# Tile order and lane placement in the recurrent tails of a hybrid decoder layer (HGRN2 and gated DeltaNet)

## The chip, the cores and the metric

The kernel runs on one core of one Trainium2 chip. Its time is the device time of one execution in microseconds; a lower time is better. Before the change three runs gave 1239.63, 1239.65 and 1236.88 us, median 1239.63. The engines are TensorE (PE), VectorE (DVE), ScalarE (ACT), GpSimd (POOL) and SyncE (SP), which issues most of the DMAs.

## The reference

One decoder layer is computed for a prompt of 512 tokens and for 8 sampled sequences of 4 tokens (32 sample tokens), with shared weights. The mixer projects the input once and splits it among four groups of heads of width 256: block-sparse attention, Mamba-2, HGRN2 and gated DeltaNet. Their outputs are concatenated, go through one output projection, then follow cross-attention over 256 memory tokens and a SwiGLU block. The two recurrences that the change touches are:

```python
# HGRN2 (gla_chunked), one chunk
bcum = jnp.cumsum(gc, axis=1)
o = (jnp.einsum('blsh,bshv->blhv', att, vc)
     + jnp.einsum('blhk,bhkv->blhv', qc * jnp.exp(bcum), S))
S = (jnp.exp(b_last[:, 0])[..., None] * S
     + jnp.einsum('bshk,bshv->bhkv', kc * jnp.exp(b_last - bcum), vc))
# gated DeltaNet (gated_delta_chunked), one chunk; t_mat is a triangular inverse
v_new = u - jnp.einsum('bhlk,bhkv->bhlv', w, S)
o = (jnp.einsum('bhls,bhsv->blhv', qk, v_new)
     + jnp.einsum('blhk,bhkv->blhv', qc * jnp.exp(gam)[..., None], S))
S = jnp.exp(gam_h[:, :, -1])[..., None, None] * S + jnp.einsum('blhk,bhlv->bhkv', k_dec, v_new)
```

The prompt starts from a zero state; each sampled sequence starts from its own state, which is updated and returned.

## The kernel before

All 544 tokens lie side by side in the free dimension, features in the partitions. TILES cuts them into four prompt tiles of 128 tokens (0 to 3) and the sample tile of 32 tokens (4). The program of each engine is written out by hand in stages: inputs, win, ssm, gdn, wout, cross, wxo, wdn. There is no scheduler: every engine runs its instructions in the order of the code, and semaphores carry the waits between engines. Inside a stage several generators run as lanes, and a string of letters says whose step comes next on PE, DVE and ACT alike.

The ssm stage has the lanes m (Mamba-2, then HGRN2), p (the sampled attention with its pages), u (norms of the DeltaNet's q and k) and n (the Mamba norm). LANES orders them. The third step of n on DVE (ssm_norm_vector, L2165) scales Mamba's output, two instructions of 128x544; its other steps on DVE are empty. A step of p on DVE ends the softmax of the sampled attention: a reduce, a reciprocal and two scalings (L1726 to L1730), for whose result PE waits. HGRN2 computes its attention matrix by levels (j = 0 to 7): DVE scales q and k, PE multiplies, DVE places the result (place, L2348). Then comes HGRN's tail: h_kd, the decayed k, and v are turned by PE (turn, L2467) into banks 0 and 1, ACT copies them (kept), PE multiplies k and v into a state contribution (added) and the outputs (output), DVE updates the state (state, L2548). The tail takes the tiles in the order 0, 1, 4, 2, 3. The banks 0 and 1 also hold level products, hence the waits on h_lv_out.

The gdn stage begins with gdn_tensor (L2800): for each tile, products of k with k and q; DVE masks them with decays (L2706 to L2726). Between two tiles hgrn_norm_tensor (L2265) sums the squares of HGRN's outputs per head, eight PE records (an fp32 product leaves two records in the trace); it needs ACT's two squares of those outputs. Then the triangular inverses are built, a dense exchange between PE, DVE and ACT. Last comes the DeltaNet tail (gdn_tail_tensor, L2877, gdn_tail_vector, L2965), lane t, interleaved with lane k, the projection of the memory tokens to K and V: 16 GEMM steps of 24 products each, then 4 steps in which K is turned (four transposes and one ACT copy each). GDN_LANES is "tk" three times, "tkk" seven times, then "tkkk". A tile takes two t steps on PE: in the first the state is applied to the keys (tail_w) and the next tile is turned, in the second come v_new, DVE's copy of it, and then state contribution and outputs. For the sample tile the state is one per sequence: 32 products of 4 columns for tail_w, 32 more for the outputs; DVE expands v_new to one block per sequence (4 instructions of 32x512, tail_vm), and PE multiplies it in four products of 512 columns into banks 4 and 7.

G_TURNS orders the tiles 0, 4, 1, 2, 3. The four sample products of 512 columns stand behind an extra yield, so two GEMM steps run ahead of them:

```python
if x == 2:
    turn(x + 1)
yield
if sample:
    pe.wait_ge(S("tail_vm"), 3)
```

After the stage all engines meet: the wout stage is entered when PE, DVE and ACT have ended gdn.

Of the kernel before, what the change touches and what calls it, by code (L numbers as in the profile page):

```python
# [19 lines left out]
ALU = mybir.AluOpType  # L20
# [47 lines left out]
def build(nc, a, o):  # L68
# [12 lines left out]
    with ctx:  # L81
# [2252 lines left out]
        def hgrn_vector(v):  # L2334
# [112 lines left out]
        H_PLACED = sum(len(H_JOBS[j]) for j in (*range(H_PACKED), 7))  # L2447
# [18 lines left out]
        def hgrn_tail_tensor(pe):  # L2466
            def turn(i):  # L2467
                t0, w, _ = TILES[i]
                x = H_AT[i]
                if x >= 2:  # L2470
                    pe.wait_ge(S("tail_tok_out"), x - 1)
                else:
                    pe.wait_ge(S("h_lv_out"), H_PLACED - len(H_JOBS[7]) + x + 1)
# [15 lines left out]
            def output(i):  # L2489
# [4 lines left out]
                if i == 0:  # L2494
                    pe.wait_ge(S("h_lv_out"), H_PLACED)
# [49 lines left out]
        def hgrn_vector_tail(v):  # L2545
            yield
# [253 lines left out]
        def gdn_tensor(pe):  # L2800
            pe.wait_ge(S("tail_tok_out"), NT)
            pe.wait_ge(S("states_made"), 2)
            for i, (t0, w, _) in enumerate(TILES):
# [12 lines left out]
                if i == 2:  # L2816
                    hgrn_norm_tensor(pe)
# [57 lines left out]
        G_TURNS = (0, 4, 1, 2, 3)  # L2875

        def gdn_tail_tensor(pe):  # L2877
            def turn(x):

                t0, w, _ = TILES[G_TURNS[x]]  # L2880
                sl = slice(t0, t0 + w)
                b_ = bank((0, 7)[x % 2])
                if x == 3:
                    pe.wait_ge(S("states_made"), 3)
# [10 lines left out]
            for x, i in enumerate(G_TURNS):  # L2895
                t0, w, _ = TILES[i]
# [3 lines left out]
                if i and not sample:  # L2900
                    pe.wait_ge(S("tail_state"), 5 + i)
# [18 lines left out]
                if x != 2 and x + 1 < NT:  # L2920
                    turn(x + 1)
                yield
                pe.wait_ge(S("tail_tok_out"), 5 + x + 1)
# [8 lines left out]
                pe.wait_ge(S("tail_vn_out"), x + 1)  # L2932
                if not sample:
                    if i == 1:
                        pe.wait_ge(S("states_made"), 3)
# [17 lines left out]
                if x == 2:  # L2953
                    turn(x + 1)
                yield
                if sample:
# [4 lines left out]
                    last.then_inc(S("tail_st"), 1)  # L2961

        t_rt = sm(2, NS)

        def gdn_tail_vector(v):  # L2965
            yield
            for x, i in enumerate(G_TURNS):
                t0, w, _ = TILES[i]
                sl = slice(t0, t0 + w)
                sample = w == NS  # L2970
                tokens = bank((0, 7)[x % 2])
                v.wait_ge(S("tail_tok"), 5 + x + 1)
                V.tensor_copy(t_tok[0:w, 0:256], tokens[0:w, 0:256])
                if sample:
                    v.wait_ge(S("tail_w"), 1)
# [3 lines left out]
                elif i:  # L2979
                    link(V.tensor_copy(t_tok[0:w, 256:512], tokens[0:w, 256:512]))  # L2980
                    v.wait_ge(S("tail_w"), i + 1)
# [7 lines left out]
                v.wait_ge(S("tail_vn"), x + 1)  # L2989
# [625 lines left out]
```

## Time and profile before

| What | Value |
|---|---|
| time, median of 3 runs | 1239.63 us |
| time of the profiled execution | 1239.63 us |
| its span | 1238.0 us, 24845 instructions |
| DVE busy | 598.7 us (48%) |
| ACT busy | 448.9 us (36%) |
| POOL busy | 441.0 us (36%) |
| chain that ended last, by engine | PE 74%, DVE 12%, issue 4%, ACT 4% |
| HBM read, written | 131.64 MB, 10.20 MB |
| HGRN tail | about 412 to 428 us |
| start of the DeltaNet stage, up to the first inverse product | 428 to 438.6 us |
| DeltaNet tail with the memory K/V product | 481.6 to 566.4 us |

The profile is one execution recorded by the hardware profiler. Its span is the time between its first and last recorded instruction, and lies 1.6 us under the time of the same execution. Times of rows are microseconds from the span's start. PEld is TensorE's weight load, which overlaps its products. PEclk is the clock that was granted to TensorE as a share of full speed: 1.00 is 2.4 GHz, 0.50 is 1.2 GHz. A line number such as L706 can be that of a helper: L264 is every product, L267 every transpose, L706 every tensor_tensor of DVE.

### The profile page before, as it was taken

To read this page: it belongs to the slowest core of one execution; us is meant where nothing else is said; L and a number is where in the kernel's file an instruction comes from. 1 tells how busy PE (TensorE), PEld (TensorE's weight loads), DVE (VectorE), ACT (ScalarE), POOL (GpSimd) and SP (SyncE) were. 2 spreads that over 40 slices of the span, in tenths; PEclk is the share of its full clock that TensorE was granted. 3 is DMA by queue.
4 is the path that set the end of the run, shared out by engine and by line. 5 is a ranking of instruction groups with operands and counts; after the bars stand their busy time and mean duration, and the time that the engine had idled before them with its cause. 6 is when DMAs were issued, how large, how long until landed. Compare 5 with 4: busy or idle time off the path is not lost.

```text
span 1238.0 us, 24845 instructions
## 1 busy us (share of the span) xinstructions
PE 1166.6 (94%) x10272; PEld 1014.0 (82%) x10272; DVE 598.7 (48%) x1068; ACT 448.9 (36%) x802; POOL 441.0 (36%) x370
## 2 busy tenths in 40 slices
PE   7999999988988988998989899999999999999998
PEld 6999997855655688887989656988999999977775
DVE  5699735236478886413291463184433334321003
ACT  6323234245544444233552342454222223221212
POOL 8433533053417121452603200614434444433331
PEclk9999999989979998898998899999999999999999
DMA  6332523066659422336414753312222232232221
GB/s 161 91 86 69 175 74 121 2 202 183 192 156 329 134 80 81 104 107 211 120 35 141 235 174 115 104 51 86 86 86 87 85 100 82 75 103 71 83 85 72
DMA packets 176581, 143.45 MB, mean 116 GB/s; under 512 B 15955, under 2 KB 162820, under 8 KB 176214
## 3 DMA queue, kind: packets, MB, share of 16 engines
q1 hardware_dynamic: 166838, 120.44, 32.5%
q0 software_dynamic: 7200, 20.23, 5.4%
q8 instruction: 81, 1.33, 0.5%
q10 hardware_dynamic: 2432, 1.21, 0.3%
q14 instruction: 30, 0.25, 0.1%
HBM read 131.64 MB, written 10.20 MB: 115 GB/s over the span
## 4 chain that ended last, share of the span: by engine, by line
PE 74%; DVE 12%; issue 4%; ACT 4%; POOL 2%; DMA 1%; SPq 1%; POOLq 0%; DVEq 0%; ACTq 0%
PE PS L264 67%; PE PS L267 7%; DVE SC L706 2%; DVE PROJ L1939 2%; POOL W_LO L248 2%; DVE XN L936 1%; DVE XT L706 1%; DVE PROJ L2358 1%; SPq L536 1%; DVE XN L706 1%; DVE XN_parts L926 1%; ACT PROJ L1342 1%; DVE PROJ L706 1%; ACT W_HI L239 0%; DVE PROJ L1940 0%
## 5 line engine op out<-in xcount | busy, mean ns | idle before, releaser
L248 POOL TENSOR_TENSOR W_LO<-W,W_HI 128x1024 fp32r<-128x1024 f32 x128 | 313.8, 2456 | 635.1 <-ACT W_HI L239 634.9
L264 PE MATMUL PS<-XN_parts,W_HI 128*128 128x272 f32 x1184 | 340.6, 288 | 0.0
L264 PE MATMUL PS<-OM_parts,W_HI 128*128 128x272 f32 x960 | 277.3, 289 | 0.0
L264 PEld LDWEIGHTS PS<-XN_parts,W_HI 128*128 128x128 f32 x1184 | 223.2, 188 | 0.0
L239 ACT ACTIVATE W_HI<-W 128x1024 fp32r<-128x1024 f32 x128 | 134.2, 1054 | 209.5 <-PE PS L264 209.5
L264 PE MATMUL PS<-OM_parts,W_LO 128*128 128x272 f32 x704 | 203.9, 290 | 0.0
L264 PE MATMUL PS<-SC_parts,W_HI 128*128 128x272 f32 x608 | 179.9, 296 | 3.9 <-POOL W_LO L248 3.2
L264 PEld LDWEIGHTS PS<-OM_parts,W_HI 128*128 128x128 f32 x960 | 181.8, 189 | 0.1
L264 PE MATMUL PS<-SC_parts,W_LO 128*128 128x272 f32 x608 | 176.8, 291 | 0.0
L264 PEld LDWEIGHTS PS<-OM_parts,W_LO 128*128 128x128 f32 x704 | 132.3, 188 | 0.0
L264 PEld LDWEIGHTS PS<-SC_parts,W_HI 128*128 128x128 f32 x608 | 115.6, 190 | 8.3 <-issue 6.1
L264 PEld LDWEIGHTS PS<-SC_parts,W_LO 128*128 128x128 f32 x608 | 115.4, 190 | 0.0
L264 PE MATMUL PS<-W_HI,PROJ_parts 128*128 128x512 f32 (+1 forms) x320 | 110.6, 374 | 0.0
L264 PE MATMUL PS<-W_HI,SC_parts 128*128 128x256 f32 (+1 forms) x288 | 87.3, 337 | 0.0
L264 PEld LDWEIGHTS PS<-W_HI,PROJ_parts 128*128 128x128 f32 x320 | 60.9, 190 | 13.3 <-issue 2.8
L706 DVE TENSOR_TENSOR SC<-SC 128x272 f32<-128x272 f32 (+6 forms) x68 | 37.2, 550 | 50.3 <-ACT SC L866 41.1
L264 PE MATMUL PS<-OM_parts,PROJ_parts 128*128 128x272 f32 x256 | 54.7, 303 | 5.9 <-DVE XN_parts L926 3.7
L264 PEld LDWEIGHTS PS<-W_HI,SC_parts 128*128 128x128 f32 x288 | 53.1, 197 | 8.4 <-issue 4.1
L264 PE MATMUL PS<-W_LO,SC_parts 128*128 128x512 f32 (+1 forms) x160 | 58.4, 365 | 0.0
L706 DVE TENSOR_TENSOR SC<-PS,RSQ 128x544 f32<-128x544 f32 x22 | 15.9, 724 | 87.1 <-PE PS L264 85.2
L3410 ACT ACTIVATE SC<-SC 128x544 f32<-128x544 f32 x22 | 14.5, 658 | 114.9 <-DVE SC L706 114.9
L1342 ACT ACTIVATE PROJ<-PS 128x512 f32<-128x512 f32 x68 | 40.1, 598 | 40.3 <-PE PS L267 40.3
(405 smaller groups left out, 2073.7 us busy)
## 6 DMA issues: line engine op xcount, KB each, us to landing
W<-in_w_gu SPq DMA_DIRECT2D x44, 512.0 KB, 3.9
W<-in_w_in SPq DMA_DIRECT2D x30, 512.0 KB, 3.8
W<-in_w_down SPq DMA_DIRECT2D x22, 512.0 KB, 3.7
W<-in_w_xkv SPq DMA_DIRECT2D x16, 512.0 KB, 3.7
W_scratch<-in_cache_moba_v SPq DMA_DIRECT2D x36, 128.0 KB, 4.8
W_scratch<-in_cache_moba_v POOLq DMA_DIRECT2D x36, 128.0 KB, 4.9
XT<-in_cache_moba_k SPq DMA_DIRECT2D x32, 128.0 KB, 2.8
XT<-in_cache_moba_k POOLq DMA_DIRECT2D x32, 128.0 KB, 2.4
```

Of the source, the lines that this page charges most:

```text
L239: nc.scalar.activation(hi_lo(n)[0], raw_chunk(n), ACT.Copy)\
L248: nc.gpsimd.tensor_tensor(hi_lo(n)[1], raw_chunk(n), hi_lo(n)[0].bitcast(F32), ALU.subtract).then_inc(S("weights_split"), 1)
L264: return nc.tensor.matmul(out, lhsT, rhs, start=start, stop=stop, skip_group_check=True)
L267: return nc.tensor.transpose(out, in_, ident[0:k, 0:k])
L536: sp.dma_start(dst, src).then_inc(S(name), 16)
L706: return V.tensor_tensor(out, x, y, op)
L926: V.scalar_tensor_tensor(lo(k)[:, TOKENS[run][j]], XT[:, k, TOKENS[run][j]], par(GAINS[run][1] + k), hi(k)[:, TOKENS[run][j]].bitcast(F32) ...
L936: last = V.scalar_tensor_tensor(xn[:, k, c_], xn[:, k, c_], par(GAINS[run][0] + k), rsq[:, c_], ALU.mult, ALU.mult)
L1342: return A.activation(o_, i_, ACT.Copy)
L1939: V.scalar_tensor_tensor(dst[:, d:SEQ], src[:, 0:SEQ - d], wt[3 - d], dst[:, d:SEQ], ALU.mult, ALU.add)
L2358: V.copy_predicated(h_store(i, w), level.bitcast(I32), src).then_inc(S("h_lv_out"), 1)
L3410: A.activation(f_g[:, t % 2, :], f_g[:, t % 2, :], ACT.Silu).then_inc(S("ff_silu"), 1)
```

## The change

The change makes four edits; the number and the shapes of all products and vector instructions stay the same.

1. In HGRN's level loop the multiply h_kd = hk * h_d moves from ahead of the placement of level 7 to behind it and behind the two subtractions on the table lev. PE's waits on h_lv_out in the tail go, as tail_prep now comes after all placements.
2. In LANES the third step of the Mamba norm moves two main steps forward, directly ahead of the step that ends the softmax of the sampled attention.
3. hgrn_norm_tensor stands behind tile 0 of gdn_tensor and no longer behind tile 2.
4. The DeltaNet tail takes the tiles in the order 0, 1, 2, 3, 4. The sample tile's state products stand directly behind its outputs, without a yield ahead of them, and DVE's scaling of the sample states stands behind the wait for those products. The waits on states_made in PE's program go.

The core of the diff:

```diff
@@ hgrn_vector
-                if j == 7:
-                    v.wait_ge(S("tail_ebd"), 1)
-                    tt(h_kd, hk, h_d, ALU.mult).then_inc(S("tail_prep"), 1)
@@ hgrn_tail_tensor, turn and output
-                else:
-                    pe.wait_ge(S("h_lv_out"), H_PLACED - len(H_JOBS[7]) + x + 1)
-                if i == 0:
-                    pe.wait_ge(S("h_lv_out"), H_PLACED)
@@ hgrn_vector_tail
+            v.wait_ge(S("tail_ebd"), 1)
+            tt(h_kd, hk, h_d, ALU.mult).then_inc(S("tail_prep"), 1)
             yield
@@ gdn_tensor
-                if i == 2:
+                if i == 0:
                     hgrn_norm_tensor(pe)
@@ gdn_tail_tensor
-        G_TURNS = (0, 4, 1, 2, 3)
-                if x == 3:
-                    pe.wait_ge(S("states_made"), 3)
-            for x, i in enumerate(G_TURNS):
+            for i, (t0, w, _) in enumerate(TILES):
-                if x != 2 and x + 1 < NT:
-                    turn(x + 1)
+                if i + 1 < NT:
+                    turn(i + 1)
-                    if i == 1:
-                        pe.wait_ge(S("states_made"), 3)
-                if x == 2:
-                    turn(x + 1)
-                yield
                 if sample:
                     pe.wait_ge(S("tail_vm"), 3)
...
                     last.then_inc(S("tail_st"), 1)
+                yield
@@ gdn_tail_vector
-                yield
+                else:
+                    yield
...
+                v.wait_ge(S("tail_st"), 5 + i + 1)
                 if sample:
                     link(tt(t_s0.rearrange("p b c d -> p (b c) d"), t_s0.rearrange("p b c d -> p (b c) d"),
                             bc(t_lasts.rearrange("p b (c o) -> p (b c) o", o=1), (P, 2 * NB, DH)), ALU.mult))
-                v.wait_ge(S("tail_st"), 5 + x + 1)
-                if sample:
@@ LANES
-                         + ["u"] + ["ppppu"] * 4 + ["ppppuun"] * 2 + ["pppp", "p", "p", "np", "", "", ""])
+                         + ["u"] + ["ppppu"] * 4 + ["ppppuun"] * 2 + ["pppp", "np", "p", "p", "", "", ""])
```

On DVE, at the end of HGRN's levels: the first row with L706 and SC<-W is the making of h_kd, L2358 the placement of level 7, L2171 the Mamba norm, L1726 to L1730 the end of the sampled attention's softmax.

```order
-L706 TENSOR_TENSOR SC<-W 128x1088 [waits tail_ebd]
 L2358 COPY_PREDICATED PROJ<-CN,PS 128x512 [waits h_lv_out,h_lv_mm] x4
 L706 TENSOR_TENSOR CN<-CN 128x128 [waits h_lv_out]
 L706 TENSOR_TENSOR CN<-CN 128x128
-L1726 TENSOR_REDUCE SC<-SC 128x1 [waits satt_exp]
+L706 TENSOR_TENSOR SC<-W 128x1088 [waits tail_ebd]
+L2171 SCALAR_TENSOR_TENSOR OM<-OM,SM,RSQ 128x544 [waits tail_root]
+L2171 SCALAR_TENSOR_TENSOR OM<-OM,SM,RSQ 128x544
+L1726 TENSOR_REDUCE SC<-SC 128x1 [waits satt_exp,vector_chain]
 L1727 RECIPROCAL SC<-SC 128x1 [waits vector_chain]
 L1729 TENSOR_SCALAR W<-PS,SC 128x256 [waits ms_values_used,vector_chain]
 L1730 TENSOR_SCALAR W<-PS,SC 128x256 [waits vector_chain]
```

Three large instructions now stand between the placement and the softmax's reduce, where none stood; the two of L2171 stood further behind.

On PE, at the start of the gdn stage: 128x128 rows with XN,PROJ are the products of a tile, RSQ,CN and SC,CN with 128x272 the sums for HGRN's norm.

```order
 L264 MATMUL PS<-XN,PROJ 128x128 x3
 L264 MATMUL PS<-PROJ 128x128 x4
+L264 MATMUL PS<-RSQ,CN 128x272 [waits tail_sq]
+L264 MATMUL PS<-RSQ,CN 128x272
+L264 MATMUL PS<-SC,CN 128x272 x2
 L264 MATMUL PS<-XN,PROJ 128x128 [waits tail_state]
 L264 MATMUL PS<-XN,PROJ 128x128 x3
```

The sums, with their wait for ACT's squares (tail_sq), now stand ahead of the products of tile 1.

On PE, the sample tile of the DeltaNet tail before: 32x64 is v_new, 64x32 and 64x4 are the outputs, and what follows is the GEMM of the memory projection.

```order
L264 MATMUL PS<-XN,PROJ 32x64 [waits tail_tok_out]
L264 MATMUL PS<-XN,PROJ 32x64 x3
L264 MATMUL PS<-XT,XN 64x32 [waits tail_vn_out]
L264 MATMUL PS<-XT,XN 64x32 x3
L264 MATMUL PS<-SC,XN 64x4 x32
L264 MATMUL PS<-W_HI,PROJ_parts 128x256 [waits weights_split]
L264 MATMUL PS<-W_LO,PROJ_parts 128x256
```

And now, at the end of the stage, where 64x512 are the products for the sample states and the rows of L267 the turns of the memory keys:

```order
L267 MATMUL PS<-CN,PROJ 128x128 [waits kvm_out]
L267 MATMUL PS<-CN,PROJ 128x128 x3
L264 MATMUL PS<-XN,PROJ 32x64 [waits tail_tok_out]
L264 MATMUL PS<-XN,PROJ 32x64 x3
L264 MATMUL PS<-XT,XN 64x32 [waits tail_vn_out]
L264 MATMUL PS<-XT,XN 64x32 x3
L264 MATMUL PS<-SC,XN 64x4 x32
L264 MATMUL PS<-SC,XN 64x512 [waits tail_vm]
L264 MATMUL PS<-SC,XN 64x512 x3
L267 MATMUL PS<-CN,PROJ 128x128 [waits kvm_out]
L267 MATMUL PS<-CN,PROJ 128x128 x3
```

The sample tile moved from between GEMM steps to between the turns, and its 64x512 products, which wait for DVE (tail_vm), follow its outputs directly.

## Rows read from the trace of the kernel before

**Rows 1.** The page, part 1: busy time and share of each engine.
```profile
PE 1166.6 (94%) x10272; PEld 1014.0 (82%) x10272; DVE 598.7 (48%) x1068; ACT 448.9 (36%) x802; POOL 441.0 (36%) x370
```

**Rows 2.** Chain that ended last, HGRN tail: start us, us, engine, tile, line.
```profile
413.09 2.57 DVE PROJ L2358 x4
...
417.24 0.49 DVE W L1730
...
417.78 0.92 PE PS L264 x24
...
423.36 3.29 PE PS L264 x32
```

**Rows 3.** Timeline, HGRN tail: start us, us, engine, line, operation, out<-in, count.
```profile
411.89 1.28 DVE L706 TENSOR_TENSOR SC<-W 128x1088 f32<-128x1088 f32 x1
...
414.23 0.44 PE L267 MATMUL PS<-CN,SC 128*128 128x128 f32 x2
...
419.66 1.48 DVE L2171 SCALAR_TENSOR_TENSOR OM<-OM,SM,RSQ 128x544 f32<-128x544 f32 x2
```

**Rows 4.** Chain that ended last, start of the DeltaNet stage.
```profile
431.53 4.29 PE PS L264 x40
...
438.59 4.63 PE PS L264 x88
```

**Rows 5.** Timeline, start of the DeltaNet stage.
```profile
429.33 0.64 ACT L2772 ACTIVATE SC<-OM 128x544 f32<-128x544 f32 x1
...
432.62 1.18 PE L264 MATMUL PS<-RSQ,CN 128*128 128x272 f32 x4
...
433.65 1.08 PE L264 MATMUL PS<-SC,CN 128*128 128x272 f32 x4
...
435.94 1.18 DVE L706 TENSOR_TENSOR PROJ<-SC,PS 64x256 f32<-64x256 f32 x3 [0.54 <-PE PS L264]
```

**Rows 6.** Windows: stretch, its us, busy us per engine, PEclk, DMA share, GB/s.
```profile
414.75:418.20 3.45, 2.42 (x40) 1.74 (x40) 3.04 (x10) 1.94 (x4) 0.00 (x0) 1.00 0.38 105
...
438.60:442.00 3.40, 3.40 (x64) 3.40 (x64) 2.99 (x10) 3.30 (x6) 0.00 (x0) 0.51 0.57 181
476.20:479.60 3.40, 2.18 (x32) 1.90 (x32) 2.32 (x5) 3.12 (x7) 0.00 (x0) 1.00 0.02 5
479.60:486.45 6.85, 6.00 (x31) 5.84 (x32) 3.44 (x9) 3.47 (x9) 0.00 (x0) 0.50 0.59 150
...
506.90:510.30 3.40, 2.90 (x67) 2.56 (x65) 2.05 (x3) 1.06 (x1) 3.21 (x2) 1.00 0.12 22
510.30:517.20 6.90, 6.90 (x54) 6.88 (x51) 4.36 (x5) 0.64 (x2) 1.25 (x1) 0.51 0.44 144
...
568.10:575.20 7.10, 6.41 (x26) 5.52 (x26) 5.88 (x9) 3.16 (x6) 0.00 (x0) 0.52 1.02 330
```

**Rows 7.** Chain that ended last, DeltaNet tail.
```profile
508.68 21.76 PE PS L264 x200
...
533.01 6.34 PE PS L264 x56
...
539.93 7.81 PE PS L264 x64
```

**Rows 8.** Timeline: products, VectorE and ScalarE work of the two tails.
```profile
424.69 1.93 PE L264 MATMUL PS<-PROJ,SC 32*64 32x512 f32 x8
...
498.68 2.03 PE L264 MATMUL PS<-SC,XN 64*64 64x4 f32 x64
...
508.66 4.63 DVE L706 TENSOR_TENSOR SC<-XN,CN 32x512 f32<-32x512 f32 x4
...
513.47 1.22 DVE L706 TENSOR_TENSOR XN<-XN,SM 128x1024 f32<-128x1024 f32 x1
...
521.96 1.28 DVE L706 TENSOR_TENSOR XN<-XN,PS 128x512 f32<-128x512 f32 x2 [7.27 <-PE PS L264]
...
565.79 0.60 ACT L3119 ACTIVATE PROJ<-PS 128x512 f32<-128x512 f32 x1 [0.26 <-PE PS L267]
```

More of the change, by code:

```diff
@@ L2446, in build @@
         H_TURNS = (0, 1, 4, 2, 3)
-        H_PLACED = sum(len(H_JOBS[j]) for j in (*range(H_PACKED), 7))
         H_AT = {i: x for x, i in enumerate(H_TURNS)}
@@ L2873, in gdn_tensor, with turn @@
             mem_turn_tensor(pe)
-        G_TURNS = (0, 4, 1, 2, 3)
         def gdn_tail_tensor(pe):
-            def turn(x):
-                t0, w, _ = TILES[G_TURNS[x]]
+            def turn(i):
+                t0, w, _ = TILES[i]
                 sl = slice(t0, t0 + w)
-                b_ = bank((0, 7)[x % 2])
-                if x == 3:
-                    pe.wait_ge(S("states_made"), 3)
+                b_ = bank((0, 7)[i % 2])
                 for k in range(2):
@@ L2899, in gdn_tail_tensor @@
                 state = t_st[i % 2]
-                if i and not sample:
+                if i:
                     pe.wait_ge(S("tail_state"), 5 + i)
@@ L2919, in gdn_tail_tensor @@
                     last.then_inc(S("tail_w"), 1)
-                if x != 2 and x + 1 < NT:
-                    turn(x + 1)
+                if i + 1 < NT:
+                    turn(i + 1)
                 yield
-                pe.wait_ge(S("tail_tok_out"), 5 + x + 1)
+                pe.wait_ge(S("tail_tok_out"), 5 + i + 1)
                 for h in range(H):
@@ L2931, in gdn_tail_tensor @@
                 last.then_inc(S("tail_vn"), 1)
-                pe.wait_ge(S("tail_vn_out"), x + 1)
+                pe.wait_ge(S("tail_vn_out"), i + 1)
                 if not sample:
-                    if i == 1:
-                        pe.wait_ge(S("states_made"), 3)
                     for h in range(H):
@@ L2966, in gdn_tail_vector @@
             yield
-            for x, i in enumerate(G_TURNS):
-                t0, w, _ = TILES[i]
+            for i, (t0, w, _) in enumerate(TILES):
                 sl = slice(t0, t0 + w)
                 sample = w == NS
-                tokens = bank((0, 7)[x % 2])
-                v.wait_ge(S("tail_tok"), 5 + x + 1)
+                tokens = bank((0, 7)[i % 2])
+                v.wait_ge(S("tail_tok"), 5 + i + 1)
                 V.tensor_copy(t_tok[0:w, 0:256], tokens[0:w, 0:256])
                 if sample:
-                    v.wait_ge(S("tail_w"), 1)
+                    v.wait_ge(S("tail_w"), i)
                     tt(t_rt, gv[:, :, sl], bank(1)[:, 0:2 * w].rearrange("p (c l) -> p c l", l=w), ALU.subtract).then_inc(S("tail_rt"), 1)
@@ L2980, in gdn_tail_vector @@
                     link(V.tensor_copy(t_tok[0:w, 256:512], tokens[0:w, 256:512]))
-                    v.wait_ge(S("tail_w"), i + 1)
+                    v.wait_ge(S("tail_w"), i)
                     for e in range(2):
@@ L2988, in gdn_tail_vector @@
                 yield
-                v.wait_ge(S("tail_vn"), x + 1)
+                v.wait_ge(S("tail_vn"), i + 1)
                 V.tensor_copy(t_vn[0:w, :], bank(2)[0:w, 0:256]).then_inc(S("tail_vn_out"), 1)
                 if sample:
-                    v.wait_ge(S("tail_vn_out"), x + 1)
+                    v.wait_ge(S("tail_vn_out"), i + 1)
                     vm4 = t_vm[0:w, :].rearrange("p (h b d) -> p h b d", b=NB, d=DH)
@@ L3013, in gdn_tail_vector @@
                     last.then_inc(S("states_made"), 1)
+                    v.drain().then_inc(S("tail_state"), 1)
                 else:
@@ L3024, in gdn_tail_vector @@
                     outputs()
+                if sample:
+                    yield
         MEM_BANKS = (3, 6, 1, 5)
```

3 lines of the change are left out of this document (1 added, 2 removed).

## The prediction

> **What bounds the kernel now.** I read the busy shares first: TensorE (PE) is busy 94% of the span [rows 1], so time is saved or lost only where PE waits, or where its clock falls. The chain that ended last, read next, gives 74% to PE and 12% to VectorE (DVE), so a DVE step counts where the chain runs over it. The change touches three stretches, and I read each there: the HGRN tail (about 412 to 428 us), the start of the DeltaNet stage (428 to 439 us) and the DeltaNet tail, which runs interleaved with the memory K/V product (494 to 566 us).
>
> In the first, the chain goes over DVE's level-7 placing (L2358), the two scalings of the sampled attention's probabilities (the second is L1730), and from 417.78 on over PE almost without a break to the last HGRN state [rows 2]. In the second, PE carries the chain from 431.53 for 4.29 us, and DVE's masking of tile 3 starts at 435.94 only when PE's products of that tile are there [rows 4, 5]. In the third, the chain is PE except for short DVE copies [rows 7]: the GEMM steps cover everything else. Last I read the granted clock: PE mostly has 1.00 (2.4 GHz), but there are stretches at 0.50 to 0.52 (1.2 GHz), each behind a stretch in which PE was partly idle or ran very small products [rows 6]. One of them, 6.90 us at 0.51 from 510.3 on, follows the sample tile of the DeltaNet tail and lies on dense GEMM.
>
> **The change part by part.** The sum is made against the profiled execution, 1239.63 us (span 1238.0), which equals the median of the runs shown.
>
> *HGRN tail.* The multiply that makes h_kd (1.28 us) goes from ahead of the four placements (2.57 us) and the two lev subtractions to behind them. For whatever comes after all of these on DVE that is a swap and costs nothing. PE's turns, which stood at 414.23 [rows 3], need h_kd and now start near 411.9 + 2.6 + 0.5 + 1.3 = 416.4. They would run 1.1 us, their copies another 0.6 us, and PE would be through the first products and the third turn at about 419. The other edit, in the lane table, puts the two Mamba norm scalings (1.48 us together, at 419.66) ahead of the reduce that leads to L1730. Before, they ran while PE was busy with products; now L1730 ends 1.5 to 1.7 us later, at about 419.4 instead of 417.73. PE has the products of those probabilities in its queue there, with added(1), turn(2), turn(3), output(1), output(4), output(2) and the sample states behind them: the chain from 417.78 on is PE's own [rows 2], so nothing behind takes the delay up. DVE has 1.48 us less to do later, but is waiting for PE there. Term: +1.6. Bounds: +0.9, if PE uses its short idle moments between 414.2 and 417.8 (it was busy 2.42 us of 3.45 [rows 6]); +1.8 at the other end.
>
> The delayed turns open a gap: PE has nothing from about 414.3 to 416.4. Between 414.75 and 418.20 its busy time falls from 2.42 us to about 1.5 us. A comparable stretch with 2.18 of 3.40 us was followed by 6.85 us at half clock [rows 6]. If the clock falls here too, the following 3.4 to 6.9 us of small products run slower. Bounds 0 and +3.4 (what the fall at 510.3 cost, worked out below); as the present stretch with 2.42 us was not punished and this one would be thinner, I take a half chance of a short fall: +0.7.
>
> *Head norm sums at tile 0 instead of tile 2.* PE's eight records of sums against blk64 run from 432.62 to 434.7 [rows 5], 2.0 us. They need ACT's second square, which ends at 429.97 [rows 5]. Placed behind tile 0, PE reaches them at 428.9, waits 1.1 us for ACT and works 2.0 us, to 432.0; tile 1's products then end at 433.1 instead of 430.4. DVE finished tile 0 at 431.5, so it now idles 1.6 us ahead of tile 1; before, it idled 0.5 us ahead of tile 3 [rows 5], which goes. Net +1.1, and 0.1 for the last links: term +1.2. Behind the waiting PE instruction stand the products of tiles 1 to 4 and the whole triangular inversion, on which DVE and ACT wait in turn, so nothing takes it up before the chain's next PE piece at 438.59 [rows 4]. Bounds +0.5 (ACT's squares earlier relative to PE) and +1.6 (the gap before tile 3 stays).
>
> *DeltaNet tail, the sample tile last.* Instructions are the same; what lies beside them differs.
>
> (a) The stretch from 508.68 holds 200 PE records in 21.76 us [rows 7]. Its parts at full clock, from rows: 72 small records at the rate of 64 in 2.03 us [rows 8] = 2.3; two GEMM steps with a first product (56 records) 6.34; two steps with the v_new products (64 records) 7.81 [rows 7]; four state products of 512 columns (8 records) 1.93 [rows 8]. Sum 18.4, so the low clock cost 3.4 us. In the new order prompt tiles stand there, as they do from 530 on, where the chain shows no such slowing. Term: -3.4. Bounds -3.4 and 0.
>
> (b) The sample tile's expansion of v_new takes DVE 4.63 us [rows 8]. Before, two GEMM steps stood in PE's queue ahead of the state products that wait for it. Now they stand directly behind the 36 output products (2.3 + 0.1 us), with no step between: PE waits 4.63 + 0.05 - 2.4, term +2.2. Behind that wait stand three of the four turns of the memory keys. Bounds +2.0 and +2.8 (DVE's copy and semaphore added).
>
> (c) The small products and the wait now make some 5.9 us of thin work (v_new 0.65, copy 0.5, outputs 2.4, wait 2.3) close to the end of the stage. The same small products with GEMM around them were enough for the fall at 510.3 (PE busy 2.90 of 3.40 us ahead of it [rows 6]). So I expect the clock to fall by the time the 512-column products run, 1.93 us at full clock and twice that at half; the turns add a little. Bounds 0 and +2.4; I take +1.5, nearer the upper end. The stage change is slow anyway: 568.10 to 575.20 was at 0.52 [rows 6], and the fall there only comes earlier, not in addition.
>
> (d) The last DVE work of the stage is now the scaling of the sample states (1.22 us), behind the state products, and two additions (1.28 us) [rows 8]: 2.6 us. Beside them PE and ACT do three turns and their copies, from 563.8 to 566.38 (the last is the row at 565.79 [rows 8]), also 2.6 us. Term +0.1, bounds 0 and +1.2. The output DMA of the sample states is issued later, but ACT waits for it only behind its wout parts, over 10 us into the next stage; SP and GpSimd have the same order as before.
>
> Sum: 1.6 + 0.7 + 1.2 - 3.4 + 2.2 + 1.5 + 0.1 = +3.9 us: 1239.6 + 3.9 = **1243.5 us**.
>
> One rule of the Trainium skill bears on the gap of the first part. The trace: from 414.75 to 418.20 a good part of PE's work was transposes (L267 turns), and the clock behind it stayed at 1.00 [rows 6]. The page "TensorE: Matmul & The Clock Gate", section "Part 4: PE-mode transpose", says that transposes don't count as PE activity in the way that products do. By that rule the stretch before was thinner than its 2.42 us look, and should have been followed by a fall already; the trace does not bear it out for this stretch. By the page's rule the delayed turns would not save the clock either, and the sum would be 1239.6 + 3.9 - 0.7 + 3.4 = 1246.2, the second rival below.
>
> **The rivals.** *1, not slower: one fall of the clock for two.* The stretch at 510.3 goes (-3.4) and the sample tile's fall merges with the slow stretch that the stage change has anyway, so that (c) is 0 and the HGRN gap has no price. Then 1.6 + 1.2 - 3.4 + 2.2 + 0.1 = +1.7: 1241.3 us. For it speaks that the fall at the stage change came 2 us behind its last PE work, against it that the thin stretch is longer than 5 us. It decides when the clock falls behind the 512-column products and not ahead of them.
>
> *2, slower still: the clock falls in the new gap of the HGRN tail* and stays low through small products on which the chain runs: +3.4 for +0.7, 1246.2 us. For it: the stretch at 476.2 [rows 6]. Against it: the delay is only 2 us and PE's queue behind it is dense.
>
> *3: the fall at 510.3 only moves.* It follows the small products, but if some other alignment of prompt tiles brings one, (a) is worth 0: up to 1247. I give this with rival 2.
>
> *4, clearly faster:* two slow stretches go (also the one at 479.60, 6.85 us at 0.50 [rows 6], if the later arrival shortens it by half, -2) while HGRN costs only its lower bound: 0.9 + 0.5 - 3.4 - 2 + 2.2 = -1.8, 1237.8; even this needs luck to pass the limit below.
>
> **How the numbers follow.** The runs shown spread over 2.8 us, and what this measurement can tell from no change is about 0.3%, 3.7 us: slower means above 1243.3, faster below 1235.9. Forecast (1242 to 1245.5, two thirds of it above the limit): 0.43. Rival 1 (1240 to 1242.5): 0.29. Rivals 2 and 3 (1245.5 to 1249): 0.20. Rival 4: 0.08, half of it below the limit. Slower: 0.43 x 0.67 + 0.20 = 0.49, and 0.03 of rival 1's upper edge for scatter, 0.52. Faster 0.04, same 0.44. The range that leaves out 2 in 10 would be 1239.5 to 1248; the bounds of (c) and of the gap together widen it at the top: 1239 to 1249.
>
> **What would show it.** In the changed profile: L1730 ends about 1.6 us later relative to the start of the level-7 products; the sums against blk64 stand between tiles 0 and 1, with an idle PE before and an idle DVE behind; no half clock between the first and second prompt tile of the DeltaNet tail; a PE wait of about 2.2 us on DVE ahead of the 64x512 products at its end; a low clock that starts there. The prediction is wrong if PE shows no wait ahead of those products, if the chain from L1730 to the last HGRN state is shorter than before, or if a slow stretch of 6.9 us still lies on the K/V product.

## The result and the profile after

| | before | after |
|---|---|---|
| median of 4 runs | 1238.26 us | 1252.53 us |
| their range | 1235.94 to 1239.65 us | 1249.01 to 1257.14 us |
| profiled execution, span | 1239.63, 1238.0 us | 1254.52, 1252.8 us |
| mean granted clock in it | 0.969 | 0.956 |

The ratio is 1.0116 (95% interval 1.0080 to 1.0153). By these medians the change costs about 14 us; the forecast was 1243.5 us with a range up to 1249, so it was wrong in size, though not in sign. The four runs of before lie low: over the 99 runs of that kernel that were made with the experiments its mean is 1241.7 us, and against it the cost is 11 to 13 us.

The changed kernel was profiled a second time with the experiments, in an execution that took 1246.18 us (span 1244.5). The two profiles of one and the same program are the best guide to what happened, so both are shown from here on as A (1254.52 us) and B (1246.18 us).

To see where the time went, I cut each execution at four places that all three have: DVE's work ahead of the level-7 placement, the first product of the triangular inverses, the first turn of the DeltaNet tail, and DVE's first step in the output projection. In the chain of waits of before the second is the row at 438.59 of [rows 4]; the others:

```profile
407.75 1.30 DVE SC L706
...
481.56 4.50 PE PS L267 x20
...
566.45 1.30 DVE SC L706
```

In A these places are 408.80 (a row of its timeline, as its chain runs over PE there), 450.99, 495.29 and 584.11. Its chain:

```profile
450.99 11.24 PE PS L264 x272
...
495.29 4.50 PE PS L267 x20
...
572.20 4.64 DVE SC L706 x4
576.88 3.67 PE PS L264 x8
580.56 2.87 PE PS L267 x12
584.11 1.30 DVE SC L706
```

And of B, where the first place has this row and the others follow:

```profile
406.43 1.30 DVE SC L706
...
441.02 5.79 PE PS L264 x104
446.85 5.41 PE PS L264 x168
...
484.25 3.83 PE PS L267 x20
...
561.61 4.64 DVE SC L706 x4
566.30 3.68 PE PS L264 x8
569.98 2.80 PE PS L267 x12
573.47 1.30 DVE SC L706
```

The differences give the time of each stretch:

| Stretch | before | A | B |
|---|---|---|---|
| up to the level-7 placement | 407.75 | 408.80 | 406.43 |
| HGRN tail and start of gdn | 30.84 | 42.19 | 34.59 |
| triangular inverses | 42.97 | 44.30 | 43.23 |
| DeltaNet tail | 84.89 | 88.82 | 89.22 |
| everything behind | 671.55 | 668.69 | 671.03 |
| span | 1238.00 | 1252.80 | 1244.50 |

The tail costs 4 us in both. The HGRN tail with the start of gdn costs 3.8 us in B and 11.4 us in A, though the instructions are the same. The timeline of PE in A tells why (the columns are those of [rows 3]):

```profile
417.45 0.44 PE L267 MATMUL PS<-CN,SC 128*128 128x128 f32 x2 [2.07 <-DVE SC L706]
...
430.73 3.68 PE L264 MATMUL PS<-PROJ,SC 32*64 32x512 f32 x8
...
439.21 2.18 PE L264 MATMUL PS<-RSQ,CN 128*128 128x272 f32 x4
441.18 2.02 PE L264 MATMUL PS<-SC,CN 128*128 128x272 f32 x4
...
450.99 1.22 PE L264 MATMUL PS<-CN,XN 64*64 64x64 f32 x18 [2.41 <-DVE XT L706]
...
563.58 2.03 PE L264 MATMUL PS<-SC,XN 64*64 64x4 f32 x64
...
576.88 3.67 PE L264 MATMUL PS<-SC,XN 32*64 32x512 f32 x8 [2.29 <-DVE SC L706]
```

and in B:

```profile
414.92 0.44 PE L267 MATMUL PS<-CN,SC 128*128 128x128 f32 x2 [2.58 <-DVE SC L706]
...
425.81 1.93 PE L264 MATMUL PS<-PROJ,SC 32*64 32x512 f32 x8
...
431.13 1.18 PE L264 MATMUL PS<-RSQ,CN 128*128 128x272 f32 x4 [0.56 <-ACT SC L2766]
432.15 1.08 PE L264 MATMUL PS<-SC,CN 128*128 128x272 f32 x4
```

The eight 32x512 records take 1.93 us in B and before [rows 8], 3.68 us in A; the head-norm sums take 2.1 us in B and 4.0 us in A. That is half clock. The windows of A (us; PE busy and records; granted clock; DMA share; GB/s) show where it lay:

```profile
414.33:417.45 3.12, 1.05 (x21) 1.00 0.60 173
419.10:426.10 7.00, 7.00 (x70) 0.51 0.00 0
426.30:428.60 2.30, 2.30 (x70) 1.00 0.03 7
429.70:443.20 13.50, 13.23 (x68) 0.50 0.33 101
450.00:457.00 7.00, 6.01 (x110) 0.51 0.01 2
503.30:566.00 62.70, 60.31 (x592) 1.00 0.37 111
566.50:570.00 3.50, 3.50 (x20) 0.58 0.81 227
576.00:590.00 14.00, 10.73 (x33) 0.51 0.48 165
```

and those of B:

```profile
411.90:414.92 3.02, 0.44 (x10) 1.00 0.61 170
415.50:419.00 3.50, 3.41 (x29) 0.51 0.00 0
419.40:431.00 11.60, 10.90 (x182) 1.00 0.06 6
553.00:555.50 2.50, 2.18 (x67) 1.00 0.09 27
555.50:559.10 3.60, 3.60 (x19) 0.53 0.75 211
562.00:565.50 3.50, 2.02 (x66) 1.00 0.02 5
565.50:573.00 7.50, 6.46 (x20) 0.54 0.28 79
576.00:583.00 7.00, 5.76 (x27) 0.51 0.94 369
```

Both begin with the new gap (1.05 of 3.12 us busy, 0.44 of 3.02) and a fall right behind it. In B the clock is back after 3.5 us and stays at 1.00 up to 439.0, 2 us ahead of the first inverse product, where 6.8 us at half clock begin; in A there are 20 us at half clock from 419 to 443, where before had none up to 438.5. In the DeltaNet tail the stretch that before had at 510.3 [rows 6] is gone (503.3 to 566.0 at 1.00), as forecast. But its end now has 17 us at half clock: first 3.4 us on the K/V product behind the sample tile's first products of 4 columns (the row at 563.58 in A), at 566.5 in A and 555.5 in B; then from 576.0 in A and 565.5 in B on, over the 32x512 products, the last turns and the stage change. Before had there the 7.1 us at 0.52 alone [rows 6].

### The profile page after: what moved, and what is told of

The parts are those of the page before. It is cut to its first block, busy times and chain, and to the rows that moved or that the text cites. A ratio compares the mean times of both kernels' runs of the same rounds, so it can differ in the third digit from the quotient of the medians.

```text
span 1252.8 us, 24846 instructions
## 1 busy us (share of the span) xinstructions
PE 1179.3 (94%) x10272; PEld 1021.3 (82%) x10272; DVE 601.2 (48%) x1068; ACT 449.1 (36%) x802; POOL 442.2 (35%) x370
## 4 chain that ended last, share of the span: by engine, by line
PE 75%; DVE 12%; issue 4%; ACT 4%; POOL 2%; DMA 1%; SPq 1%; POOLq 0%; DVEq 0%; ACTq 0%
PE PS L264 67%; PE PS L267 8%; DVE SC L706 3%; POOL W_LO L248 2%; DVE PROJ L1939 1%; DVE XN L936 1%; DVE XT L706 1%; DVE PROJ L2358 1%; SPq L536 1%; DVE XN_parts L926 1%; DVE XN L706 1%; DVE PROJ L1940 1%; DVE PROJ L706 1%; ACT PROJ L1342 1%; ACT W_HI L239 0%
## 5 line engine op out<-in xcount | busy, mean ns | idle before, releaser
L264 PEld LDWEIGHTS PS<-W_HI,PROJ_parts 128*128 128x128 f32 x320 | 61.0, 191 | 13.6 <-issue 3.2
L706 DVE TENSOR_TENSOR SC<-SC 128x272 f32<-128x272 f32 (+6 forms) x68 | 37.2, 550 | 50.3 <-ACT SC L866 41.1
L706 DVE TENSOR_TENSOR SC<-PS,RSQ 128x544 f32<-128x544 f32 x22 | 15.9, 724 | 87.1 <-PE PS L264 85.2
```

Source lines behind the costliest of these rows:

```text
L264: return nc.tensor.matmul(out, lhsT, rhs, start=start, stop=stop, skip_group_check=True)
L706: return V.tensor_tensor(out, x, y, op)
```

## The experiments

**How the runs were read.** Each run gives its time, its span and its mean granted clock, so the time at half clock is 2 x (1 - clock) x span. It varies from run to run of one kernel (before: 83.4 us on average, standard deviation 7.9, over 99 runs, two identical entries counted once), and the run's time goes with it. One line per kernel with a common slope fits all 270 runs of this case (one run of 2174 us left out) to 1.3 us: **each us at half clock goes with 0.36 +- 0.01 us of time**. The table splits each kernel's mean difference to before into the part at equal half-clock time (waits; in rows with added products it holds their work too) and 0.36 times the difference in half-clock time. The price is an average over all stretches, so a fall at one particular place can cost more or less than the split says.

| Kernel | ratio to before, 95% | us at half clock | waits | clock part |
|---|---|---|---|---|
| before | 1 | 83.4 | 0 | 0 |
| edit 1 alone | 1.0021 (1.0003 to 1.0039) | 84.3 | +2.7 | +0.4 |
| edit 2 alone | 1.0046 (1.0029 to 1.0062) | 93.1 | +2.5 | +3.5 |
| edit 3 alone | 1.0015 (0.9989 to 1.0040) | 86.8 | +1.6 | +1.2 |
| edit 4 alone | 1.0018 (0.9999 to 1.0037) | 86.4 | +2.1 | +1.1 |
| edits 1, 2 | 1.0044 (1.0025 to 1.0063) | 87.5 | +2.7 | +1.5 |
| edits 1, 2, 3 | 1.0039 (1.0008 to 1.0069) | 87.0 | +3.4 | +1.3 |
| edits 1, 2, 4 | 1.0045 (1.0019 to 1.0072) | 92.3 | +2.9 | +3.2 |
| edits 3, 4 | 1.0051 (1.0029 to 1.0074) | 92.9 | +2.9 | +3.4 |
| whole change, first | 1.0116 (1.0080 to 1.0153) | 100.9 | +4.6 | +6.3 |
| whole change, again | 1.0125 (1.0089 to 1.0160) | 106.1 | +4.9 | +8.2 |
| + products in gap 1 | 1.0108 (1.0075 to 1.0141) | 105.6 | +4.7 | +8.0 |
| + products in gap 2 | 1.0078 (1.0050 to 1.0106) | 88.9 | +7.3 | +2.0 |
| + products in gap 3 | 1.0099 (1.0075 to 1.0124) | 90.0 | +8.0 | +2.4 |
| + products in all three | 1.0094 (1.0060 to 1.0128) | 78.3 | +11.6 | -1.8 |
| whole change, tail covered | 1.0099 (1.0062 to 1.0137) | 98.8 | +3.8 | +5.5 |
| edit 4, tail covered | 1.0072 (1.0046 to 1.0099) | 96.0 | +1.9 | +4.5 |
| before + products | 1.0003 (0.9979 to 1.0027) | 69.9 | +5.3 | -4.8 |

The waits are good to about 0.4 us, 0.6 us where a kernel has 6 runs; the mean half-clock time only to 2 to 5 us with 8 to 20 runs and 2 to 7 us with 6.

**Edit 1 alone.**

```diff
-                if j == 7:
-                    v.wait_ge(S("tail_ebd"), 1)
-                    tt(h_kd, hk, h_d, ALU.mult).then_inc(S("tail_prep"), 1)
...
         def hgrn_vector_tail(v):
+            v.wait_ge(S("tail_ebd"), 1)
+            tt(h_kd, hk, h_d, ALU.mult).then_inc(S("tail_prep"), 1)
             yield
```

> Edit 1 alone: h_kd is made behind the level-7 placement and the two lev subtractions; the Mamba norm stays where it was. Both theories see PE idle for about 2 us ahead of the HGRN turns. Clock theory (the 14.3 us of the whole change are mostly half-clock time, started by that gap): the granted clock falls to 0.50 within some 2 us behind the turns and stays there for 7 to 17 us, so the low-clock total of the trace (77.8 us of half clock before) rises by 7 to 17 us and the time by 3 to 8 us. Wait theory (the terms of the prediction without the clock): a swap on DVE, +0.0 to +1.1 us.

**Edit 2 alone.**

```diff
-                         + ["u"] + ["ppppu"] * 4 + ["ppppuun"] * 2 + ["pppp", "p", "p", "np", "", "", ""])
+                         + ["u"] + ["ppppu"] * 4 + ["ppppuun"] * 2 + ["pppp", "np", "p", "p", "", "", ""])
```

> Edit 2 alone: the Mamba norm's two scalings stand ahead of the softmax's end on DVE. L1730 ends 1.5 to 1.7 us later. Wait theory: +1.6 us. Clock theory: PE's gap here is in another place (ahead of the products of the probabilities, 417.2 to 419.3), with the turns and first products done before; the clock may fall too: +1.6 to +5 us.

**Edits 1 and 2 together.**

> Edits 1 and 2 together on the kernel before (the expanded h_kd late, the LANES Mamba norm early), edits 3 and 4 left out. Alone they gave 1.0021 and 1.0046. Wait theory (both delay the same products of the HGRN tail, so their waits overlap): at an equal time at half clock 2 to 3 us over the kernel before, not the 4.8 that the sum of the two would be. Clock theory: the two together stretch the gap in which PE is idle, so that the time at half clock is 8 to 15 us over that of before (82.9), worth 3 to 5 us; ratio 1.004 to 1.007. Rival, the waits add up: ratio 1.0067 with no more time at half clock than edit 2 alone has (93).

Each alone costs 2.5 to 2.7 us of waits, and so do the two together: both hold up the same products, one through the turns of h_kd, the other through L1730. The rival that they add up fell. Their time at half clock (87.5) came out below the 91 to 98 that the clock theory asked for. For edit 1 both theories missed: its time at half clock rose by 1 us and not by 7 to 17, and its waits are 2.7 us and not at most 1.1.

The traces say more on these 2.7 us. From DVE's row at 407.75 (its like in each kernel) to the start of HGRN's eight 32x512 records it is 16.94 us before, 19.86 with edit 1 and 19.81 with edits 1 and 2. Both have a fall of 3.4 us behind the gap. The part of it from the making of h_kd on takes 12.63 or 12.64 us there, and 11.10 in the one profile with edits 1 and 2, and nothing added, that has full clock over all of it (the covered tail, below). So the wait alone is about 1.4 us, and the fall adds about 1.5. The fall is no accident of these two: it comes 0.5 us ahead of the turns' start to 1.6 us behind it in 7 of the 9 profiles that have edit 1 and nothing in the gap, and in none of the 7 without edit 1. Of the two exceptions one has a gap of only 0.92 us. That the total at half clock hardly rises with edit 1 is not explained.

**Edit 3 alone.**

```diff
-                if i == 2:
+                if i == 0:
                     hgrn_norm_tensor(pe)
```

> Edit 3 alone: HGRN's norm sums behind tile 0. Wait theory: +1.2 us (DVE idle 1.6 us ahead of tile 1). Clock theory: the same, plus or minus a half-clock stretch of 3.4 us (1.0 to 1.7 us of time) at the first inverse products: +0 to +3 us.

1.6 us of waits. The traces agree: from the start of HGRN's eight 32x512 records to that of the sample tile's first products of gdn (64x32) it is 11.24 or 11.25 us in the executions without edit 3 (before, edit 1, edit 2, edits 1 and 2), and 12.37 or 12.38 us in those with it (edit 3, edits 3 and 4, B), all of them executions in which the eight records took 1.93 to 1.96 us: +1.13. They show a second effect that no theory had: the half clock around the first inverse product lasts 6.8 us in 7 of the 8 profiles with edit 3 and nothing added there, and 3.4 us in all 7 without it. At the average price that is 1.2 us more.

**Edit 4 alone.**

```diff
-        G_TURNS = (0, 4, 1, 2, 3)
...
+            for i, (t0, w, _) in enumerate(TILES):
```

> Edit 4 alone: the DeltaNet tail in the order 0, 1, 2, 3, 4. Wait theory: +2.3 us for the wait on the expanded v_new and the last states, no more. Clock theory: the half-clock stretch at 510 goes (-3.4) and one comes at the end of the stage, longer than before: sum +0.5 to +3 us. Both nearly agree in time; the traces tell them apart: whether half clock lies on the 64x512 products and how long the low stretch at the stage change is (7.1 us before, 14 us with the whole change).

2.1 us of waits, what the new wait ahead of the last products was put at; nothing of a net gain by the clock. The profile of it has the 3.67 us records in the HGRN tail too, where it changes nothing: this fall comes to a kernel without edits 1 to 3 as well. It is in 5 of the 11 profiles with edit 1 and in 1 of the 7 without; so few don't show that edit 1 makes it more frequent.

**The change without one of its parts.** Without edit 4, without edit 3, without edits 1 and 2:

> The change without edit 4 (DeltaNet's tail in its old order). Clock theory: the waits of edits 1 to 3 lie in one place (HGRN tail and the start of the gated-delta stage) and join two half-clock stretches into one; time at half clock 95 to 100 us, ratio 1.007 to 1.010, most of the whole change's 1.0116. Wait theory: 3.5 us at equal clock, ratio 1.003 to 1.005, and edit 4 would then be worth more in company than its 1.0018 alone.

> Edits 1, 2 and 4: the change without the head-norm sums at tile 0. Theory, the clock falls more often only where the gap at the start of the gated-delta stage is widened by all of edits 1 to 3 and the tail then runs in edit 4's order: at equal clock 4.5 us over before minus 1 for edit 3, time at half clock near 87, ratio 1.004 to 1.006. Rival, edit 4's tail in company with edits 1 and 2 is enough: time at half clock near 100, ratio 1.008 to 1.011.

> Edits 3 and 4: the change without the two edits of the HGRN tail. Theory, most of the added half clock lies between 419 and 443 us and needs edits 1 and 2: about 3 us at equal clock, time at half clock 84 to 90, ratio 1.002 to 1.005. Rival, edits 3 and 4 between them carry it: time at half clock near 100, ratio 1.007 to 1.010.

No part carries the half-clock time: 87, 92 and 93 us, each 9 us or more short of the whole's. Nor is more than their sum needed: the four single edits add 0.9, 9.7, 3.4 and 3.0 us at half clock, together 17.0 with an error of about 6, the whole 18.7. In time, edits 1 and 2 (+4.2 us) and edits 3 and 4 (+6.3) add up to 10.5 of the whole's 11 to 13. The whole, run once more beside the last two, came out as at first:

> The changed kernel once more, so that the partial kernels of this group are compared with it on one chip, and for a second profile. If the 1.0116 of the first comparison holds: 1.009 to 1.014 with about 100 us at half clock. If the time at half clock comes out near 87, as in the change without edit 4, the ratio is 1.005 to 1.007 and part of the first comparison was the clock's run-to-run spread.

**Products that nobody reads, in the gaps.** A helper issues products into a bank that is free there; they leave the output as it is. In the changed kernel they stand ahead of the turns in the HGRN tail (gap 1), ahead of the wait for the first inverse product (gap 2) and ahead of the wait for the expanded v_new (gap 3).

```diff
+        def keep_busy(n, b):
+            for _ in range(n):
+                mm(bank(b), ident, keep[:, 0:512], True, True)
...
+                    keep_busy(5, 1)
                     pe.wait_ge(S("tail_vm"), 3)
```

> The changed kernel with products added whose results nobody reads, each 128x512 float32 of about 0.43 us: 4 ahead of the HGRN tail's turns, 5 ahead of the first inverse product's wait, 5 ahead of DeltaNet's wait for the expanded v_new. Clock theory: these gaps are what the clock falls in, so the time at half clock drops from about 101 to 80 to 92 us, and the time by 2 to 6 us against the changed kernel (ratio to the kernel before 1.006 to 1.010). Wait theory: the gaps end when they did, the clock costs nothing, so the time is that of the changed kernel (1.0116) or up to 4 us over it where the added products outlast a gap.

> The changed kernel with two unread products of 128x512 ahead of the HGRN tail's turns alone, about 0.9 us of work in a wait of 2.07 us. Clock theory with the fall at 419 us as its first link: time at half clock 10 to 20 us below that of the changed kernel in this group, time 2 to 5 us below it. Wait theory or another first link: no change in either.

> The changed kernel with 5 unread products of 128x512 ahead of the first inverse product's wait alone. If this gap is what the falls at the start of the stage belong to: time at half clock 85 to 92 us against about 103, and with 2 to 5 us of added work the time stays within 2 us of the changed kernel's. If not: time at half clock near 103 and the time 2 to 5 us over the changed kernel's, ratio 1.013 to 1.016.

> The changed kernel with 5 unread products of 128x512 ahead of DeltaNet's wait for the expanded v_new alone, which lasts 2.3 us. If the falls at the end of the DeltaNet tail belong to this wait: time at half clock 92 to 98 us against about 103, time 1 to 3 us under the changed kernel's. If not: the same time at half clock, time 0 to 2 us over the changed kernel's.

With all three the half-clock time falls from 102 us (mean of the 26 runs of the whole change) to 78, with gap 2 or gap 3 alone to 89 and 90, with two products in gap 1 not at all. So falls of the clock do belong to gaps 2 and 3. The profiles bear it out for what stands right behind them: the half clock at the first inverse products is gone in all three kernels with gap 2 filled, and in both with gap 3 filled the 32x512 products and the turns behind them run at full clock. In the profile with gap 1 filled the fall right behind the turns is missing too, but 13.6 us at half clock come from 426.5 on. The time follows only a little: gap 2 alone gives a ratio of 1.0078 for the 1.0116 and 1.0125 of the whole, and the intervals overlap. The gain is small since five products last longer than was planned. The timeline of PE with gap 2 filled:

```profile
441.21 0.32 PE L264 MATMUL PS<-XN,PROJ 64*32 64x32 f32 x8 [0.63 <-DVE XT L706]
441.36 0.29 PE L264 MATMUL PS<-PROJ 64*32 64x32 f32 x8
441.58 4.56 PE L264 MATMUL PS<-CN 128*128 128x512 f32 x10
```

and its windows:

```profile
423.50:441.50 18.00, 15.38 (x236) 1.00 0.42 122
441.50:487.00 45.50, 40.83 (x1131) 1.00 0.08 26
```

The products take 4.56 us (10 records, where 5 were reckoned with) in a gap of 2.4 us, and behind them the clock is 1.00 up to 487, where A had 7 us at 0.51 at this place. That overrun is the +2.7 of waits. In gap 3 they last as long, over a wait of 2.3 us; the waits rose by 3.3 us there, 1 us more than this overrun, within the error.

In the kernel before, with five ahead of the first inverse product and four at the stage change:

> The kernel before with the same kind of unread products: 5 ahead of the first inverse product's wait, 4 at the change to the output projection of DeltaNet. Clock theory: the half-clock stretches at 438.5 and 568 us shorten or go, time at half clock from 82.9 to 70 to 78 us, ratio 0.997 to 0.999. Wait theory: no gain, ratio 1.000 to 1.003.

The half clock fell by 13.5 us, worth 4.8, and the added products cost 5.3: no gain.

**The end of the tail covered.** Two GEMM steps are put back between the sample tile's outputs and its 32x512 products, in the changed kernel and with edit 4 alone.

```diff
                 if sample:
+                    yield
                     pe.wait_ge(S("tail_vm"), 3)
...
-        GDN_LANES = "tk" * 3 + "tkk" * 7 + "tkkk"
+        GDN_LANES = "tk" * 6 + "tkk" * 4 + "tkk" + "tkkkk"
```

> The changed kernel with two GEMM steps of the memory K/V product between the sample tile's outputs and its state products of 512 columns (the tiles stay in the order 0, 1, 2, 3, 4; the earlier tiles get one step less each to make room). Wait theory: the wait of 2.3 us ahead of those products goes and nothing else, so 2 us under the changed kernel, ratio 1.009 to 1.011. Clock theory: the half clock on those products and on the turns behind them goes too, 5 to 10 us less of it, so 4 to 6 us under the changed kernel, ratio 1.006 to 1.008. Rival, the fall only moves: it follows the sample tile's small products wherever they stand; then as the wait theory.

> The same two GEMM steps with edit 4 alone on the kernel before. Edit 4 alone gave 1.0018, 2.1 us at equal clock. Expected: the 2.1 us go, ratio 0.999 to 1.000; with the fall at the sample tile gone too, 0.996 to 0.998, faster than both kernels. Rival, the fall only moves or prompt tiles with one GEMM step less bring new waits: 1.000 to 1.003.

The rival held: the fall moves. PE's timeline in the changed kernel with the cover:

```profile
553.56 2.79 PE L264 MATMUL PS<-SC,XN 64*64 64x4 f32 x64
...
564.46 1.93 PE L264 MATMUL PS<-SC,XN 32*64 32x512 f32 x8
```

and its windows:

```profile
544.50:554.00 9.50, 8.67 (x123) 1.00 0.39 112
554.50:561.50 7.00, 7.00 (x63) 0.51 0.48 138
562.00:571.00 9.00, 6.56 (x46) 1.00 0.31 90
571.50:578.50 7.00, 5.76 (x20) 0.51 1.00 351
```

The wait is gone and the 32x512 records run at full clock, but the clock falls during the products of 4 columns, 7 us of it now on the two GEMM steps. With edit 4 alone the cover gave 1.0072, above everything expected of it (0.996 to 1.003) and above edit 4's own 1.0018: its waits stayed (1.9 us for 2.1) and its time at half clock rose by 10 us over 6 runs. What took the place of the covered wait is not known.

## Why the prediction was wrong

In short: the waits came out as forecast, 4.7 us for 5.1. The clock did not: it was put at a gain of 1.2 us and cost about 6.7.

**Where the half clock lies.** From the windows of 0.5 us of all 18 profiles, the us at half clock by stretch. Stretch I goes from 408 to the first inverse product, II is the next 63 us, III the next 42 us (the body of the DeltaNet tail), IV the next 63 us (its end, the stage change, the start of the output projection). Of the kernels left out of the table, the covered tails have 13.7 (whole change) and 17.1 (edit 4) in IV.

| | I | II | III | IV |
|---|---|---|---|---|
| before | 0.4 | 9.9 | 6.8 | 6.8 |
| mean of the 6 without edit 4 or added products | 8.0 | 10.5 | 6.8 | 4.5 |
| A, B | 22.5, 5.0 | 16.1, 12.1 | 0, 0 | 17.1, 17.1 |
| gap 1, gap 2 filled | 16.1, 4.4 | 16.1, 6.8 | 0, 0 | 17.1, 17.1 |
| gap 3, all filled | 17.9, 2.1 | 16.2, 6.8 | 0, 0 | 10.2, 10.2 |
| edit 4; 1, 2, 4; 3, 4 | 10.8, 21.9, 3.3 | 10.2, 10.2, 12.4 | 0, 0, 0 | 17.1, 17.1, 17.1 |

III and IV are steady: edit 4 takes all of III away and sets IV to 17.1 us in every profile in which the end of the tail was left as it is. I and II vary. Part of I is not the change's: in the profiles of edit 2, of edit 3 and of edits 1, 2, 4 it holds 7.7, 7.7 and 11.7 us of a stretch that began at 405.5 or 406.0, ahead of everything that was moved. Outside the four stretches the profiles have 47 to 69 us at half clock (before 54, A 56, B 53).

**Term by term**, measured against the forecast:

- *HGRN tail wait, +1.6.* Right, as a wait: from DVE's row at 407.75 to L1730 it was 9.49 us before; in A it is 10.93, in B 10.78: +1.44 and +1.29. The forecast saw the turns come late too, but gave them no price beside L1730's delay: edit 1 alone leaves L1730 in its place (9.57 us) and costs as much as both edits.
- *Head-norm sums, +1.2.* Right: +1.13, as shown under edit 3. PE's wait for ACT is 0.56 us in B and not the 1.1 reckoned, since PE reaches the sums later than reckoned. The longer half clock at the first inverse products was not in the forecast.
- *(b) Wait for the expanded v_new, +2.2.* Right: in both A and B PE waits 2.3 us there. *(d) +0.1*: not to be told apart.
- All waits together: 5.1 forecast, 4.6 +- 0.4 and 4.9 +- 0.6 measured at equal clock.
- *(a) The stretch at 510.3 goes, -3.4.* The stretch goes, in all profiles with the new order. III held 6.8 us on average; at the average price of 0.36 that is -2.4. The stretch itself was fully busy (6.90 of 6.90 us [rows 6]), so its own price may well have been the 3.4 us forecast, and then (c) is dearer by the same 1 us: only the sum of the two is measured.
- *(c) Low clock at the end of the tail, +1.5.* **This step failed.** The products behaved as forecast (3.67 us in A, 3.68 in B, for 1.93), but I reckoned that "the fall there only comes earlier, not in addition". It comes in addition: IV grows from 4.5 to 17.1 us, 12.6 x 0.36 = +4.5. Besides the products it covers a K/V product behind the first 4-column products, the last turns and the stage change. The stretch on the K/V product is half of what rival 3 said, that the fall at 510.3 only moves. (a) and (c) together were put at -1.9 and are +2.1. A and B agree without any average price: in the tail PE is idle 2.0 and 2.1 us longer than before, the waits, and busy 1.9 and 2.2 us longer with the same 764 records.
- *The clock in the new gap, +0.7, upper bound +3.4.* **This step failed most.** The fall behind the gap does come (in A and B, and at 417 and 420 us in the profiles of edit 1 and of edits 1 and 2; not in the one with the covered tail). By itself it costs 1.1 us in B (3.5 us at 0.51; 12.23 us from h_kd on for 11.10) and 1.5 in others, for the 0.7 at which a half chance of it was put. What was not priced is that the clock can fall again on the small products behind it, up to 20 us in I, and lies at half for 7 us around the first inverse products, where before had 3.4. A against B is 42.19 - 34.59 = 7.6 us for 17.5 us at half clock in I: twice my upper bound. Over the runs, half-clock time in all stretches is 18.7 us above that of before, +6.7 us of time; less the +2.1 of the tail, 4.6 us are left for this term. That is a subtraction: I and II can't be seen in runs without a profile, and it takes the half clock outside the four stretches to be unchanged, which is not shown. With a part for edit 3's longer stretch (1.2) in it, it is the least certain figure here.

So the waits were 5.1 and the clock was put at -1.2; measured they are 4.7 and about +6.7 (of the 11 to 13 us that the means differ by). The miss of 7.9 us in the clock is 3.9 in the new gap, 3.0 in (c) and 1.0 in (a). The second rival, "the clock falls in the new gap of the HGRN tail and stays low", named the mechanism, but with a price of 3.4 us for one fall.

The rule of the Trainium skill that I weighed ("TensorE: Matmul & The Clock Gate", section "Part 4: PE-mode transpose": transposes don't count as PE activity in the way that products do) stays undecided: in A and B the turns stand behind a gap in which PE has hardly any work, so the fall at 415.5 or 419.1 needs no such rule. Of the cost, the same page of the Trainium skill, section "Terms", puts the penalty at throttled time x (1 - K/N), where K of N clock pulses pass: half of it here. The runs give 0.36 on average. One reason is that part of such a stretch is waiting that no clock shortens (PE busy 10.73 of 14.00 us in A's last window); the fully busy stretch at 510.3 cost 3.4 of 6.9 us by the forecast's estimate, which agrees with the page.

**What stays open.** Why the clock falls on the small products from 425 us on in one execution and not in the next. It did in 6 of 18 profiles (A, edit 4 alone, edits 1 to 3, edits 1, 2, 4, gap 1 filled, gap 3 filled), each time 1 to 3 us ahead of the 32x512 records and for 10 us or more; a seventh (edit 3 alone) has 3.4 us at 426.0, over before those records start. Nothing in the order of the instructions tells them apart: A has it and B, the same program, has not. No one of the four edits is a condition for it, as it comes with edit 4 alone and without edit 4. That gap 2 filled had none is one profile, and those products stand behind the stretch. Whether the whole change has more half-clock time than its parts add up to, the runs can't tell. No version beat the kernel before.

## What to carry to other kernels

Near a gap, price the stretches of small products behind it at half clock as well, not one fall; take the spread of half-clock stretches from several executions, since one profile shows one draw. A wait that a few us of small products lead up to can cost its own length and a fall on what follows. Covering the wait alone moved the fall here; whether covering the small products too would spare it was not tried. When runs of one kernel scatter by 1%, plot their time against their mean granted clock before any stretch is explained.

## What the runs showed of the hardware

- Most of the scatter between runs on this one core goes with the granted clock: over the 99 runs of the kernel before, time and time at half clock correlate at 0.91, and behind the common line a scatter of 1.3 us is left of 3.1 us.
- A us at half clock goes with 0.36 us of time here on average, not 0.5. The fall behind the gap of the HGRN tail cost about 1.5 us for 3.4 us at half clock.
- The clock fell with PE hardly idle too: in B behind a stretch of 2.50 us of which PE was busy 2.18, nearly all of it products of 4 columns.
- A float32 product of 128x512 whose result nobody reads takes 0.91 us (4.56 us for 5, ten records) at full clock, and keeping PE busy with such products raises the granted clock behind them (half-clock time 102 to 78 us). They cost nearly as much as they give back: 6.9 us for 8.5 with all three gaps filled, 5.3 for 4.8 in the kernel before.
- Two executions of one program can differ by 8.3 us (1254.52 and 1246.18) with 7.6 us of it in one stretch of 40 us.
